# A two-layer block with expert gathers: layer 0's prologue written in an order built around tile 0

## What is computed

```
mod = silu(c) @ w_ada[l] + b_ada[l];  sh1, sc1, g1, sh2, sc2, g2 = split(mod, 6)
h = rms_norm(x, norm1_g[l]) * (1 + sc1) + sh1
p, q, k, v = split(h @ w_in[l])                 # 512, 512, 128, 128 columns
y = concat(multiscale_pool(p), sliding_window_attention(rms(q), rms(k), v))
x = x + g1 * (rms_by_half(y) * mix_norm_g[l] @ w_out[l])
h2 = rms_norm(x, norm2_g[l]) * (1 + sc2) + sh2
x = x + g2 * peer_ffn(h2)
```

## Time before, and how to read the profile

| what | value |
|---|---|
| three runs | 2814.84 us median, 2810.55 to 2817.07 |
| the profiled execution | 2813.48 us, span 2811.8 us |
| mean granted TensorE clock | 0.89 of full speed |
| busy share of the span | PE 79%, PEld 44%, DVE 49%, ACT 28%, POOL 40% |
| moved by DMA | 902.77 MB, mean 321 GB/s |

### The profile page before, as it was taken

How to read it: one execution, slowest core, us unless ns; L and a number is a source line. 1 busy time by engine, 2 the same in 40 slices (tenths; PEclk the granted TensorE clock), 3 DMA queues, 4 the chain that set the end, 5 groups by cost and what they waited for, 6 DMA issues and landing times. The chain is left out here.

```text
span 2811.8 us, 29004 instructions
## 1 busy us (share of the span) xinstructions
PE 2214.5 (79%) x8948; PEld 1223.7 (44%) x8948; DVE 1378.6 (49%) x2956; ACT 788.5 (28%) x2246; POOL 1122.9 (40%) x1249
## 2 busy tenths in 40 slices
PE   5778886676977978788777676779889987879995
PEld 2455552222333434445324232346555645646663
DVE  5656657775566484555755654433232222432222
ACT  1324323232333334343332343324110111411111
POOL 4015556667666555465566666620011110001111
PEclk9789988889988989899888889889789998879998
DMA  9548889999999999899899999952189985128996
GB/s 354 217 157 336 318 301 405 366 365 404 411 413 407 405 383 386 303 367 352 324 368 370 367 375 372 374 211 75 61 324 420 420 337 185 57 122 326 419 420 267
DMA packets 244866, 902.77 MB, mean 321 GB/s; under 512 B 25522, under 2 KB 32194, under 8 KB 222210
## 3 DMA queue, kind: packets, MB, share of 16 engines
q0 software_dynamic: 157360, 567.05, 52.8%
q1 hardware_dynamic: 87380, 334.23, 30.0%
HBM read 881.27 MB, written 19.92 MB: 321 GB/s over the span
## 5 line engine op out<-in xcount | busy, mean ns | idle before, releaser
L1490 PE MATMUL PS<-arena 128*128 128x512 f32 x2048 | 1038.5, 658 | 350.9 <-issue 169.4
L2086 DVE CUSTOM_DVE_ANT_0 JK<-arena,PS 128x1024 bf16<-128x1024 f32 x512 | 625.0, 1221 | 411.3 <-DMA arena<-in_peer_u_dram,IDX 275.8
L1490 PEld LDWEIGHTS PS<-arena 128*128 128x128 f32 x2048 | 409.8, 209 | 939.6 <-issue 876.1
L878 POOL DMA_INDIRECT arena<-in_peer_v_dram,IDX x512 | 503.9, 984 | 470.7 <-PE PS L1490 261.1
L875 POOL DMA_INDIRECT arena<-in_peer_u_dram,IDX x512 | 493.7, 964 | 335.8 <-DVE IDX L2059 162.5
L911 POOL DMA_DIRECT2D expert_rows<-mod x128 | 67.6, 529 | 640.8 <-DVE mod L2517 393.4
L1048 ACT ACTIVATE ACTV<-DOT 128x1 f32<-128x1 f32 x512 | 101.9, 199 | 756.6 <-DVE DOT L2086 474.9
L1806 PE MATMUL PS<-arena,HT 128*64 128x256 f32 x2048 | 235.1, 382 | 24.1 <-DMA arena<-in_w_down_dram 21.8
L1061 ACT ACTIVATE arena<-IDENT,GACT 128x128 f32<-128x128 f32 x512 | 205.5, 401 | 107.1 <-remote 47.7
L2543 DVE COPY mod<-PS 128x256 f32<-128x256 f32 x64 | 27.2, 425 | 330.4 <-PE PS L1806 330.4
L1806 PEld LDWEIGHTS PS<-arena,HT 128*64 128x64 f32 x2048 | 141.4, 137 | 99.4 <-DMA arena<-in_w_down_dram 26.3
(11 more groups left out here) (342 smaller groups left out, 1881.3 us busy)
## 6 DMA issues: line engine op xcount, KB each, us to landing
arena<-in_w_gate_dram SPq DMA_DIRECT2D x64, 1024.0 KB, 19.2
arena<-in_w_up_dram SPq DMA_DIRECT2D x64, 1024.0 KB, 21.8
arena<-in_w_down_dram SPq DMA_DIRECT2D x64, 1024.0 KB, 17.7
arena<-in_w_ada_dram SPq DMA_DIRECT2D x24, 2048.0 KB, 11.8
arena<-in_w_in_dram SPq DMA_DIRECT2D x11, 2048.0 KB, 16.4
arena<-in_peer_wq_dram SPq DMA_DIRECT2D x10, 2048.0 KB, 8.0
expert_rows<-mod POOLq DMA_DIRECT2D x128, 128.0 KB, 5.5
arena<-in_w_out_dram SPq DMA_DIRECT2D x6, 2048.0 KB, 8.6
```

The lines of the kernel that those rows point to most:

```text
L878: pool.indirect_dma_start(out=GV[b], out_offset=None, in_=v_rows, in_offset=off).then_inc(v_loaded[b], 16)
L1490: last = pe.matmul(PO[:, half, :], DIAG[:, n % DIAGS, :], GV[BUF[n]][:, half * 512:(half + 1) * 512], start=(j == 0), stop=False, skip_gro ...
L2086: dve.tensor_tensor_reduce(JUNK, GU[BUF[n]], HP[tt].rearrange("p b n -> p (b n)"), 1.0, 0.0, ALU.mult, ALU.add, DOT[:, s:s + 1]).then_inc( ...
```

## The change

The order of layer 0's prologue is written anew on PE, ACT and DVE, and `psum_jobs` with it; some `w_ada` sums are called in halves; and chunks 8 and 11 of `w_ada` go through slot 4 of the weights, with the slots of `wq` 0 and 2 exchanged for it. Nothing is added to the work or left out. The kernel is joined to the same second block as before.

```diff
--- before.py
+++ after.py
@@ -132,25 +132,30 @@
     halves("hT", 0, 1)
     add(("pool", 0, 0), "s")
     add(("in", 0, 1, 0), "s")
+    heads(0, 0)
     add(("mix", 0, 0), "v")
+    scores(0, 0)
     add(("in", 0, 1, 1), "s")
-    heads(0, 0)
-    scores(0, 0)
     add(("in", 0, 1, 2), "s")
+    for b in range(2):
+        add(("apT", 0, 0, b), "s")
     add(("pool", 0, 1), "s")
+    add(("apv", 0, 0), "v")
     add(("mix", 0, 1), "v")
-    values(0, 0)
     heads(0, 1)
+    halves("yT", 0, 0)
+    add(("out", 0, 0, 0), "v")
+    ada(0, 4, 4)
+    add(("out", 0, 0, 1), "v")
+    ada(0, 8, 4)
     scores(0, 1)
-    halves("yT", 0, 0)
-    ada(0, 4, 4)
-    for c in range(2):
-        add(("out", 0, 0, c), "v")
-    values(0, 1)
-    ada(0, 8, 4)
     add(("subT", 0), "s")
     halves("h2T", 0, 0)
-    query(0, 0, 0, BESIDE_TILE0)
+    add(("wq", 0, 0, 0), "s", BESIDE_TILE0)
+    for b in range(4):
+        add(("apT", 0, 1, b), "s", BESIDE_TILE0)
+    add(("s", 0, 0, 0), "s", BESIDE_TILE0)
+    add(("apv", 0, 1), "v", BESIDE_TILE0)
     query_tail(add, halves, query, 0)
 
     for j in range(SLOTS):
@@ -286,9 +291,9 @@
     *[(("ada", 0, n), "v", n) for n in range(4)],
     (("in", 0, 0), "p", 4), (("in", 0, 1), "p", 0), (("in", 0, 2), "p", 5),
     (("ada", 0, 4), "v", 1), (("ada", 0, 5), "v", 2), (("ada", 0, 6), "v", 3), (("ada", 0, 7), "v", 1),
-    (("out", 0, 0), "p", 2), (("out", 0, 1), "p", 3),
-    (("ada", 0, 8), "v", 1), (("ada", 0, 9), "v", 0), (("ada", 0, 10), "v", 1), (("ada", 0, 11), "v", 0),
-    (("wq", 0, 0), "p", 4), (("wq", 0, 1), "p", 1), (("wq", 0, 2), "p", 0), (("wq", 0, 3), "p", 2),
+    (("out", 0, 0), "p", 2), (("ada", 0, 8), "v", 4), (("out", 0, 1), "p", 3),
+    (("ada", 0, 9), "v", 0), (("ada", 0, 10), "v", 1), (("ada", 0, 11), "v", 4),
+    (("wq", 0, 0), "p", 0), (("wq", 0, 1), "p", 1), (("wq", 0, 2), "p", 4), (("wq", 0, 3), "p", 2),
     *[(("ada", 1, n), "v", n % 2 * 2) for n in range(4)],
     (("in", 1, 0, 0), "p", 0), (("in", 1, 1, 0), "p", 2), (("in", 1, 2, 0), "p", 6),
     *[(("ada", 1, n), "v", n % 2 * 2) for n in range(4, 12)],
@@ -698,7 +703,7 @@
                 if name == ("ada", 0, 4):
                     with nc.allow_non_contiguous_dma(reason="small parameter vectors"):
                         params_of_a(0)
-                if name == ("ada", 0, 8):
+                if name == ("ada", 0, 10):
 
                     used(sp, ("in", 0, 2))
                     sp.dma_start(NGAIN[0][1], row(norm2_g[0], P)).then_inc(gains_loaded, 16)
@@ -1173,29 +1178,29 @@
                 projected(0, 0, c)
             transposed("hT", 0, 1)
             pooled(0, 0)
+            head_root(0)
             projected(0, 1, 0)
-            head_root(0)
+            heads_transposed(0, 0)
+            head_exps(0, 0)
             projected(0, 1, 1)
-            heads_transposed(0, 0)
             projected(0, 1, 2)
+            probs_transposed(0, 0)
             pooled(0, 1)
-            head_exps(0, 0)
-            probs_transposed(0, 0)
             head_root(1)
             heads_transposed(0, 1)
             y_root(0)
             transposed("yT", 0, 0)
             for n in range(4, 8):
                 modulation(0, n)
-            head_exps(0, 1)
-            probs_transposed(0, 1)
             x_root(0)
             for n in (10, 11):
                 modulation(0, n)
             subkeys_transposed(0)
             transposed("h2T", 0, 0)
             h_to_psum(0, 0)
+            head_exps(0, 1)
             query(0, 0, 0)
+            probs_transposed(0, 1)
             keyed(0, 0, 0)
             y_root(1)
             query(0, 0, 1)
@@ -1584,30 +1589,30 @@
             turn_rows("hT", 0, 1)
             pool_means(0, 0)
             project_in(0, 1, 0)
+            turn_heads(0, 0)
             pool_mix(0, 0)
+            head_scores(0, 0)
             project_in(0, 1, 1)
-            turn_heads(0, 0)
-            head_scores(0, 0)
             project_in(0, 1, 2)
+            turn_probs(0, 0)
             pool_means(0, 1)
+            head_values(0, 0)
             pool_mix(0, 1)
-            turn_probs(0, 0)
-            head_values(0, 0)
             turn_heads(0, 1)
-            head_scores(0, 1)
             turn_rows("yT", 0, 0)
+            project_out(0, 0, 0)
             for n in range(4, 8):
                 modulation(0, n)
-            for c in range(2):
-                project_out(0, 0, c)
-            turn_probs(0, 1)
-            head_values(0, 1)
+            project_out(0, 0, 1)
             for n in range(8, 12):
                 modulation(0, n)
+            head_scores(0, 1)
             turn_subkeys(0)
             turn_rows("h2T", 0, 0)
             query(0, 0, 0)
+            turn_probs(0, 1)
             key_scores(0, 0, 0)
+            head_values(0, 1)
             query(0, 0, 1)
             key_scores(0, 0, 1)
             slots_of_tile0(0)
@@ -1896,7 +1901,7 @@
                         dve.wait_ge(bada_first, 16)
                     else:
                         dve.wait_ge((bada_loaded, bada_next)[l], 16)
-                w = ring[CH[name][1]].rearrange("p (k n) -> p k n", k=2)
+                w = chunk_at[CH[name][1]].rearrange("p (k n) -> p k n", k=2)
                 acc = MODL[l][:, n // 4 * 2048:(n // 4 + 1) * 2048]
                 for k in halves:
                     if k == 0:
@@ -2224,33 +2229,36 @@
                 means = MT[:, :, at:at + P]
                 dve.tensor_tensor(means, means, IDENT.unsqueeze(1).broadcast_to([P, 4, P]), ALU.subtract).then_inc(means_ready, 1)
             accumulate(0, 4)
+            accumulate(0, 5, (0,))
             head_squares(0, 0)
+            accumulate(0, 5, (1,))
             head_rows(0, 0)
+            accumulate(0, 6, (0,))
             mixed(0, 0)
-            accumulate(0, 5)
+            accumulate(0, 6, (1,))
             scored(0, 0)
-            accumulate(0, 6)
+            accumulate(0, 7)
+            accumulate(0, 8)
             head_squares(0, 1)
-            head_rows(0, 1)
-            mixed(0, 1)
-            accumulate(0, 7)
+            accumulate(0, 9, (0,))
             valued(0, 0)
             y_squares(0, 0)
+            head_rows(0, 1)
             y_rows_of(0, 0)
-            accumulate(0, 8)
-            scored(0, 1)
-            accumulate(0, 9)
+            mixed(0, 1)
+            accumulate(0, 9, (1,))
+            accumulate(0, 10)
+            accumulate(0, 11)
             taken(dve, ("ada", 0, 7))
             mixer_added(0, 0, 0)
             mixer_added(0, 0, 1)
-            accumulate(0, 10)
-            valued(0, 1)
-            accumulate(0, 11)
             for n in (8, 9):
                 gain_rows(0, n, 2)
             taken(dve, ("ada", 0, 9))
             taken(dve, ("ada", 0, 11))
             modulated(0, 0, 3)
+            scored(0, 1)
+            valued(0, 1)
             y_squares(0, 1)
             y_rows_of(0, 1)
             for part in routing:
```

## The result

| | before | changed |
|---|---|---|
| median of the runs | 2813.25 us (2810.55 to 2817.07, 4 runs) | 2785.87 us (2767.05 to 2789.98, 4 runs) |
| ratio of the two, 95% interval | | 0.9889 [0.9842, 0.9936] |
| profiled execution | 2813.48 us, span 2811.8 | 2789.98 us, span 2788.4 |
| mean granted TensorE clock | 0.89 | 0.90 |

The kernel is faster by 1.1%, 0.6% to 1.6%. The two profiled executions differ by 23.5 us, where the sum had said 22.5. As a ratio the forecast is 0.9920, inside the interval; but 0.9889 itself, on the 2813.25 of before, is 2782.0, a microsecond under the range's lower end. The ratio follows the means, 2782.2 on 2813.5, and not the medians.

The account below looks back on a forecast made before the run. The prologue was taken as in series with a transfer-bound expert loop: 29.2 us gained up to h2, 6.7 given back, first gather 22.5 earlier, so 2813.5 becomes 2791.0 us; range 2783 to 2803.

Parts of the forecast that it names:

- the sum: Whole kernel: first gather from 193.36 to 170.9, so 22.5 us off the profiled 2813.5, giving 2791.0.
- tile 1's values: PE work behind the first query, between h2 and the first gather: 5.0 us, ending at 150.2.
- The walk: Prologue's engine orders followed with durations from the old trace, up to the first gather at 170.9.
- The new wait on ACT: Before tile 0's mixer rows: y_root(0) stands behind tile 1's heads_transposed, taken as 2.5 us, bounds 1 and 4.
- the first part: Prologue up to tile 0's mixer rows, which were to end at 101.8 instead of 110.25.
- The table load: ACT ahead of tile 1's exponentials: done at 137.0, before DVE's maximum at 137.2; the skill's 1.38 us drain left out.
- Half clock: PE stays at half clock through prologue output and modulation products: 2794 to 2809, chance 0.10.
- The stream doesn't keep the gain: Expert loop: POOL waits at the fifth slot, or transfers swallow part of the earlier start; 2800 to 2812, chance 0.09.
- No effect: Another event ties the first gather, so nothing comes of the change: 2813, chance 0.03.
- slower: Prologue: a late load among chunks 8 to 11 delays DVE's last sum; 2817.3 with sums done at 151.2, chance 0.04.
- 3 for the spread of runs: Allowance of 3 us in the forecast's own range, 2785 to 2798, beside 4 us for small waits.
- the stream behind it is the same work: Expert loop after the first gather: same work in the same order, so the 22.5 us shift carries whole.

Follow-up runs that it names:

- held-back kernel: Changed kernel with idle POOL work delaying its first gather to about the old time: 2805.83 us, ratio 0.9985; on the third chip 2698.0 us, 0.9991.
- control: Copy of the kernel before, unaltered, measured against it on the third chip: 2698.56 us, ratio 0.9993.
- changed again: Changed kernel unaltered, run again on the first chip against the kernel before: 2788.2 us, ratio 0.9909.
- old slots: Changed kernel's order with the slot table of before (chunks 8 to 11 through slots 1, 0, 1, 0): 2790.92 us, ratio 0.9917 to the kernel before.
- rows first: Changed kernel with tile 0's mixer rows moved ahead of tile 1's heads: 2664.65 us, ratio 0.9895 to the kernel before; third chip 2661.07 us, 0.9873.
- slots-only kernel: Kernel before with only the new slot table (chunks 8 and 11 in slot 4, wq 0 and 2 exchanged): 2694.17 us, ratio 0.9999.
- both edits: Changed kernel with tile 0's mixer rows ahead of tile 1's heads and routing's first maximum ahead of tile 1's valued: 2663.66 us, ratio 0.9887 to before.

## Where the prediction held, and which term was mis-sized

| step | predicted, us | measured, us |
|---|---|---|
| tile 0's mixer rows end | 101.8 | 101.75 |
| first output product takes | 10.0 | 9.54 |
| four modulation products take | 3.5 | 3.60, twice |
| sums done | 114.3 | 114.39 |
| `modulated(0, 0, 3)` ends | 131.9 | 131.33 |
| exponentials end | 141.4 | 140.8 |
| PE free of the first query | 142.4 | 142.19 |
| tile 1's values take | 5.0 | 3.76 |
| tile 1's mixer rows end | 154.4 | 153.1 |
| first gather | 170.9 | 169.59 |

**The walk** held at every step and was out by 1.3 at its end, nearly all of it tile 1's values. Their 4.99 went into the sum as read from a row of before, without its clock. The windows of before over that row, and of the changed kernel over the same 32 records and one of their neighbour's:

```profile
140.60:145.60 5.00, 4.96 (x32) 4.77 (x32) 4.04 (x4) 2.43 (x4) 0.00 (x0) 0.73 0.03 5
```

```profile
145.10:148.70 3.60, 3.60 (x33) 3.60 (x33) 0.00 (x0) 1.81 (x2) 0.00 (x0) 1.00 0.00 0
```

Granted 0.73 it took 4.99, and 4.99 by 0.73 is 3.6; granted full speed it took 3.76. Before, PE had stood idle for 0.94 ahead of it; now PE comes to it from the first query with no idle time that the timeline shows. The output product had been priced with its clock in view, and was right to 0.5. The new wait on ACT is real: 2.29 idle ahead of the reciprocal at 100.14. Two small things of opposite sign hid in the first part: tile 0's `scored` began 1.35 earlier than walked (74.65 for 76.0), as `mixed` ahead of it ended at 72.16 for the 73.6 of the walk, which no row shown gives, and the first half of chunk 9 waited 1.17 for its load, which had been walked as landed.

**The table load.** ACT's timeline of the changed kernel:

```profile
134.89 1.28 ACT L1012 ACT_TABLE_LOAD   x1
136.68 0.51 ACT L1012 ACTIVATE arena<-arena,SV 128x256 f32<-128x256 f32 x1 [0.51 <-DVE SV L1979]
```

The load ends at 136.17 and the first exponential starts 0.51 later, released by DVE's maximum. By the 1.38 us of drain that the Trainium skill gives ("ScalarE: Activation LUTs", What ACT_TABLE_LOAD costs) it could not start before 137.55. The trace disagrees, and the sum was right to go without it. (The sum with it comes to 2792.2, a tenth less than the prediction says.)

**The rivals.** Half clock: refuted, 0.89 granted over the stretch. The stream doesn't keep the gain: a loss of most of it is refuted by the held-back kernel and the control, a loss of a few us is not; at the fifth slot POOL never waited for `project_out(0, 1, 1)`, which ended at 174.1. No effect and slower: both refuted, the sums being done 9.8 us ahead of the products that read them (114.39 for 124.19).

**The mis-sized term** is "3 for the spread of runs", which rested on the 6.5 us between three runs. The four changed runs lie 22.9 us apart, and the ratio of four runs to four is known to 0.0047 only, 13 us: that is what the term measured. The range ended 8 us below the forecast, and the measured ratio lies 9 below it. The prediction argued its lower end, 2783, from the modulation products and tile 1's values "all at full clock". But the sum already had the products at full clock (3.5, measured 3.60 twice), and the values gave 1.24, so this reason leads to 2789.8 and no further. Nothing was left for a run like the one of 2767.05. Whether one falls into a sample of four is chance, and so is on which side of 2783 such a ratio comes out.

By the ratios the gain was 31.2 us in the first measurement, 25.6 on repetition and 21.9 on the third chip, by the medians 27.4, 23.5 and 26.0, with the gather earlier by 23.8, 22.8 and 24.5. The forecast of 22.5 lies inside all three intervals. The mechanism held, and the size of the shift to 1.3 us. One term more was put at nothing, "the stream behind it is the same work": its first data came 1 to 2 us sooner after the first gather, as told above, and these intervals can hide as much.

What makes a low run is open: none of the changed kernel's on the first chip was traced. But it goes with the clock. In every set of runs whose clocks are on record the time falls as the mean granted clock rises, weakly in a few: 2767.05 had 0.906 where the three others had 0.900, and the other lowest runs of that chip, 2776.55 (changed again), 2776.36 (old slots), 2788.26 (held back) and 2798.06 (before), had 0.905 to 0.907, for 0.890 to 0.903 in all the rest. Which of the two follows the other is not shown. The version with the rows first gives a hint: its lowest run of the second chip was the profiled one (2647.51), and in it the stream took 1513.6 us and the rest 972.2, for 1520.5 and 978.6 in the profile of the slots-only kernel, at a mean clock of 0.932 for 0.921. These are two different kernels, but both parts behind the prologue are shorter.

First and last gather of the loop, from POOL's timelines:

| profiled execution | first gather | stream | behind it |
|---|---|---|---|
| before | 193.36 | 1648.0 | 970.4 |
| changed | 169.59 | 1650.6 | 968.3 |
| changed again | 170.52 | 1645.7 | 973.4 |
| held back, first chip | 193.31 | 1635.7 | 972.9 |
| before, third chip | 192.89 | 1521.3 | 984.0 |
| changed, third chip | 168.38 | 1518.5 | 980.8 |
| held back, third chip | 194.48 | 1517.4 | 979.7 |
| rows first, third chip | 160.38 | 1514.9 | 973.4 |

Two traces on the first chip cannot show a carried shift: the stream of equal work differs by 15 us between them, and the change's shift of -23.8 wanders between -26.2 and -14.2 along the loop. On the third chip the stream of these kernels differs by 4 us. On the second, between the kernel with both edits and the one with the slots only, the shift is -33.1 at the start, stays between -33.2 and -29.4, and is -30.9 at the end.

## What to carry to other kernels

When a prologue stands in series with a saturated stream, forecast the time of the stream's first transfer, and look at which bulk load goes out beside it; walking the engines' orders with durations from the old trace gave the first gather here to 1.3 us in 24, and every duration taken from such a row wants the clock of its stretch beside it. Ask then whether the chain has turned: after this change DVE waits for PE, so a further gain came from moving the mixer's rows ahead of other work, while an earlier gather that met a weight load gained nothing by the fourth slot. Size the range by the spread of many runs of the kernel before, not by three; and to show that a shift is what makes a gain, put the delay back and see the gain go.

## What the runs showed of the hardware that had not been expected

- The chips differ in the loop alone. In the same 400 us window the first moved 383 to 393 GB/s and the others 409 to 410; the stream took 1635.7 to 1650.6 us on the first and 1513.6 to 1522.7 on the others, while the part behind it was if anything shorter on the first (964 to 973 for 972 to 987). This row is from the windows of the kernel before on the third chip, to be held against the earlier trace rows:

```profile
400.00:800.00 400.00, 297.50 (x626) 122.01 (x627) 270.49 (x513) 138.44 (x438) 272.58 (x264) 0.90 1.03 409
```

- The spread differs as well: the kernel before ranged over 31.5 us in 18 runs on the first chip, and over 14.0 in 23 on the third.
- The nearer ahead of the first gather a weight load goes out, the later its data are used: the first dot product came 4.7 us after the first gather with the load 26.6 ahead, 6.6 to 7.0 with it 2.8 ahead, and 7.7 to 8.0 with it 1.0 or 0.0 ahead.
- A table load whose next activation waits for another engine cost nothing at all, and 0.01 us passed between a load and its activation where nothing else was waited for the earlier trace rows. The sum had taken it so; the new part is that the wait for DVE hides the load whole.
